# Softmax denominators moved from the probabilities to the outputs, by way of rows in memory, in a hybrid attention and state-space layer

## The chip, the cores and the metric

The kernel runs on one core of a Trainium2 chip. The metric is the device time of one execution in microseconds (us); lower is better.

## The reference, cut to what matters

One layer of a decoder works on 1024 prompt tokens and 8 x 4 sample tokens of width 1024. A normalised input goes through one projection, whose columns are the queries, keys and values of 16 attention heads of size 64, and the gate, the convolution input and the steps of a state-space mixer. Both mixers' outputs are joined, projected, and followed by a feed-forward part. The change touches only the prompt's attention. Its three dilated windows with merging weights amount to one softmax with a count of windows in the bias:

```python
m = jnp.max(logits, axis=-1, keepdims=True)
pr = jnp.exp(logits - m)
den = jnp.sum(pr, axis=-1)
o = jnp.einsum('gnhqk,gnkhd->gnqhd', pr, vb) / den    # per head, per query
```

The division can stand before the product with the values (on the probabilities) or behind it (on the output), since `den` belongs to a query and not to a key.

## The kernel before, in words

The program has four stages in one launch: `project` (queries, keys, values), `weave`, `mixers` (state-space scan and sample attention) and `outward` (output projection and feed-forward). The change lies in `weave`, in the ring of projection weights (`Ring`) that `weave` takes over from `project`, and in nothing else.

`weave` mixes two jobs by hand. Job one is the prompt's attention, head by head. Job two is the rest of the input projection: 20 feature tiles, 24 units of three matmuls each (`dense`, L973), the first 12 tiles followed by a four-tap convolution on VectorE (`convolve`, L1114 and L1118), all 20 by an activation (tanh on ScalarE, `gate` on VectorE, L1130). The order is written out in ticks, 12 for each head, from -9 to 193 and some more for the tail; every engine runs the same list of ticks in program order, so an instruction that waits holds up all behind it on its engine. With h the head and qt one of 8 tiles of 128 queries, a tick can hold:

- `scores(h, qt)` on TensorE (L991, L992), then `bias_min` on VectorE (L1078): adds the bias and takes each query's minimum into `att_min`; then, a tick later, `exponent` on ScalarE (L1172): the exponential with its sum into `att_den`.
- `invert` on VectorE (L1060), in the same tick as `exponent`: 96 instructions in all, each the inverse of one or two columns of `att_den`; then `normalise` on GpSimd (L920): multiplies the 128 x (128 to 1024) probabilities in place by a scalar of each query. GpSimd's queue also holds `split_part` (L233, L235), which cuts each raw weight tile into a high and a low part, two halves a tile, 3 and 5 ticks after the tile before it has begun on TensorE.
- `turn` on TensorE (L1002) transposes the probabilities; `keep_high` on ScalarE (L1180) and `keep_low` on VectorE (L1065) move them to memory in two parts; `values` on TensorE (L1017 to L1022) multiplies them with the values into one PSUM bank; `split_out` on ScalarE and `add_out` on VectorE (L1053) move the output of a half head into `att_oT`, 64 partitions a head; `store_out` on ScalarE's queue (L1203) writes a head's 64 x 1024 to memory.

Probabilities come out with queries on the partitions, so the inverse denominators are a column there. The outputs come out transposed, with queries along the free dimension, so there the same numbers must be a row, the same for all 64 partitions of a head.

SyncE's queue, also in ticks, loads keys, queries, bias, values and raw weights. Raw weights lie in a ring of two slots of 128 x 1024; tile n goes to slot n % 2 and its load waits until tile n - 2 has been split. Behind its last tick the same queue loads what `mixers` begins with (L1472, L1475, L1460 and on).

## Time and profile before

| | us |
|---|---|
| three runs | 1935.82, 1939.14 (median), 1946.28 |
| the profiled execution | 1942.02 |
| its span, first to last instruction | 1940.1 |
| stretch of `weave` in that span | about 330 to 830 |

The profile gives each engine's busy time and instructions by source line, what ended each idle time, and the chain of work that ended last. Engines: PE is TensorE's matmul, PEld its weight load, DVE VectorE, ACT ScalarE, POOL GpSimd, SP SyncE; a name with q behind it is that engine's own sequencer or queue. Granted clock is TensorE's, 1.00 being 2.4 GHz. Matmuls overlap, so their durations added up are more than the time that they take.

### The profile page before, as it was taken

How to read it: one execution, taken by the hardware profiler on the slowest of the kernel's cores; microseconds unless marked ns; L12 is line 12 of the kernel's file. 1: busy time of each engine (PE TensorE's matmuls, PEld its weight loads, DVE VectorE, ACT ScalarE, POOL GpSimd, SP SyncE). 2: the span in 40 equal slices, each digit the busy share in tenths (PEclk: the TensorE clock that was granted, in tenths of full speed). 3: DMA queues.
4: the chain of work that ended last, by engine and by line, in shares of the span. 5: the costliest groups of instructions: out<-in, count | busy, mean ns of one | idle time of the engine just before them, and what ended most of it. 6: DMA issues, size and time to landing. Idle time of an engine off the chain costs nothing.

```text
span 1940.1 us, 33409 instructions
## 1 busy us (share of the span) xinstructions
PE 1851.5 (95%) x12776; PEld 1700.9 (88%) x12776; DVE 1405.9 (72%) x1897; ACT 887.6 (46%) x1610; POOL 1099.8 (57%) x846
## 2 busy tenths in 40 slices
PE   8999999998888999989997999999999999999999
PEld 7999999887777888855556789989999999999999
DVE  5788830787677766569987655798767779877876
ACT  5433412576566777456663002343333344444442
POOL 4588740777676777424444223335555557777774
PEclk9999999999999999979998999999999999999999
DMA  4444433543443443389995535114343357444442
GB/s 172 148 169 179 172 136 94 126 130 95 109 110 95 134 125 111 113 287 327 328 319 177 185 145 189 73 61 183 123 162 144 137 212 285 149 152 156 143 134 92
DMA packets 139097, 309.31 MB, mean 159 GB/s; under 512 B 31659, under 2 KB 65323, under 8 KB 135228
## 3 DMA queue, kind: packets, MB, share of 16 engines
q1 hardware_dynamic: 114924, 270.60, 41.5%
q10 hardware_dynamic: 24016, 36.58, 5.5%
q8 instruction: 103, 1.69, 0.3%
q14 instruction: 54, 0.44, 0.1%
HBM read 222.42 MB, written 93.28 MB: 163 GB/s over the span
## 4 chain that ended last, share of the span: by engine, by line
PE 58%; DVE 11%; POOL 5%; issue 5%; ACT 3%; DMA 0%; ACTq 0%; DVEq 0%; POOLq 0%
PE ff_ps L2594 31%; PE dense_ps L973 7%; PE wo_psa L2429 5%; POOL att_p L920 3%; PE att_t_ps L1002 2%; PE wo_psb L2561 2%; PE wo_psa L2561 1%; PE att_s_ps L991 1%; PE att_s_ps L992 1%; DVE sa_vlo L1961 1%; POOL w_lo L235 1%; PE ssd_in L1638 1%; DVE silu_half L1118 1%; PE sa_s L1551 1%; DVE ssd_m L1879 1%
## 5 line engine op out<-in xcount | busy, mean ns | idle before, releaser
L2594 PE MATMUL ff_ps<-ff_set,ff_wring 128*128 128x264 f32 x5376 | 661.5, 286 | 8.4 <-DVE ff_set L3206 3.5
L2594 PEld LDWEIGHTS ff_ps<-ff_set,ff_wring 128*128 128x128 f32 x5376 | 658.9, 189 | 10.5 <-DVE ff_set L3206 3.9
L920 POOL TENSOR_SCALAR att_p<-att_p,att_rden 128x128 f32<-128x128 f32 (+7 forms) x128 | 242.3, 1901 | 118.2 <-DVE att_rden L1060 118.1
L2263 POOL TENSOR_TENSOR ff_wring<-const,ff_wring 128x256 fp32r<-128x256 f32 (+1 forms) x192 | 212.6, 1111 | 146.5 <-ACT ff_wring L2759 145.9
L2759 ACT ACTIVATE ff_wring<-const 128x256 fp32r<-128x256 f32 (+1 forms) x192 | 93.5, 489 | 222.0 <-PE ff_ps L2594 108.4
L3228 DVE TENSOR_TENSOR h<-h,ff_ps 128x528 f32<-128x528 f32 x192 | 133.2, 700 | 49.9 <-PE ff_ps L2594 47.1
L1180 ACT ACTIVATE att_pThi<-att_t_ps 128x512 fp32r<-128x512 f32 x192 | 93.5, 487 | 133.6 <-PE att_t_ps L1002 125.3
L1078 DVE CUSTOM_DVE_ANT_0 att_p<-att_s_ps,att_bias 128x128 f32<-128x128 f32 (+7 forms) x128 | 95.3, 754 | 57.8 <-PE att_s_ps L992 51.9
L1065 DVE TENSOR_TENSOR att_pTlo<-att_t_ps,att_pThi 128x512 fp32r<-128x512 f32 x192 | 104.5, 552 | 41.2 <-ACT att_pThi L1180 41.0
L973 PE MATMUL dense_ps<-u_hi,w_hi 128*128 128x352 f32 x480 | 115.0, 341 | 10.3 <-DVE conv_pre L1092 3.1
L2263 POOL TENSOR_TENSOR ff_wring<-wo_raw,ff_wring 128x256 fp32r<-128x256 f32 (+1 forms) x72 | 83.5, 1159 | 61.8 <-ACT ff_wring L2759 61.8
L680 DVE RECIPROCAL proj_rinv<-proj_rinv 128x1056 f32<-128x1056 f32 x16 | 108.1, 6753 | 9.8 <-ACT proj_rinv L570 9.8
L1002 PE MATMUL att_t_ps<-const,att_p 128*128 128x128 f32 x576 | 96.7, 277 | 13.3 <-POOL att_p L920 8.7
L973 PE MATMUL dense_ps<-u_hi,w_lo 128*128 128x352 f32 x480 | 108.8, 335 | 0.0
L973 PE MATMUL dense_ps<-u_lo,w_hi 128*128 128x352 f32 x480 | 107.7, 333 | 0.0
L1172 ACT ACTIVATE att_p<-att_p,att_min 128x128 f32<-128x128 f32 (+7 forms) x128 | 98.3, 769 | 12.9 <-DVE att_min L1078 12.5
L235 POOL TENSOR_TENSOR w_lo<-w_raw,w_hi 128x512 fp32r<-128x512 f32 (+1 forms) x52 | 100.2, 1928 | 5.4
L2253 POOL CAST wo_hi<-wo_raw 128x1024 fp32r<-128x1024 f32 x16 | 18.1, 1131 | 147.4 <-issue 83.4
L2263 POOL TENSOR_TENSOR ff_wring<-ff_raw,ff_wring 128x256 fp32r<-128x256 f32 (+1 forms) x72 | 78.0, 1083 | 40.0 <-ACT ff_wring L2759 40.0
L973 PEld LDWEIGHTS dense_ps<-u_hi,w_hi 128*128 128x128 f32 x480 | 81.2, 191 | 19.6 <-issue 11.3
L1002 PEld LDWEIGHTS att_t_ps<-const,att_p 128*128 128x128 f32 x576 | 70.4, 142 | 31.1 <-issue 20.4
L2429 PE MATMUL wo_psa<-mix_split,wo_hi 128*128 128x352 f32 x384 | 81.8, 341 | 7.3 <-DVE mix_split L2893 4.3
(366 smaller groups left out, 4316.2 us busy)
## 6 DMA issues: line engine op xcount, KB each, us to landing
tmp_r_sets<-h SPq DMA_DIRECT2D x16, 1848.0 KB, 5.9
ff_setraw<-tmp_r_sets SPq DMA_DIRECT2D x56, 528.0 KB, 5.5
sa_k<-in_cache_k SPq DMA_DIRECT2D x32, 640.0 KB, 8.9
sa_v<-in_cache_v SPq DMA_DIRECT2D x40, 512.0 KB, 4.7
w_raw<-in_w_feat SPq DMA_DIRECT2D x36, 512.0 KB, 6.4
out_qk<-proj_out SPq DMA_DIRECT2D x16, 528.0 KB, 8.0
tmp_bias_rows<-tmp_table ACTq DMA_DIRECT2D x8, 1024.0 KB
att_bias<-tmp_bias_rows SPq DMA_DIRECT2D x16, 512.0 KB, 3.4
```

The costliest lines, as they stand in the source:

```text
L235: pool.tensor_tensor(self.lo[:, j, ks, :], raw, self.hi[:, j, ks, :].bitcast(F32), ALU.subtract).then_inc(self.split, 2 // parts)
L680: dve.reciprocal(rinv[:], rinv[:]).then_inc(inverted, 1)
L920: pool.tensor_scalar(slot(h, qt), slot(h, qt), rden[:, qt, :], None, ALU.mult).then_inc(normed, 1)
L973: mm = pe.matmul(bank(acc, c, w), wt[:, j, k, :], xt[:, k, c:c + w], start=(k == 0 and p == 0), stop=(k == KD - 1 and p == 2))
L1002: mm = pe.transpose(t_ps[n % 2][:, c:c + P], slot(h, qt)[:, b * P:(b + 1) * P], kit.c(C_IDENT, P))
L1065: dve.tensor_tensor(p_lo[:, n % TURNED, off:512], t_ps[n % 2][:, off:512], p_hi[:, n % TURNED, off:512].bitcast(F32), ALU.subtract).then_i ...
L1078: dve.tensor_tensor_reduce(out=slot(h, qt), in0=s_ps[:, base:base + w], in1=bias[:, h % 2, SEQ - w:SEQ], scale=1.0, scalar=3e38, op0=ALU.a ...
L1172: act.activation(slot(h, qt), slot(h, qt), ACT.Exp, bias=low[:, qt, :], scale=-1.0, accum_out=den[:, qt, :]).then_inc(exped, 1)
L2263: pool.tensor_tensor(w_set(n)[:, 1], operand(q, m), w_set(n)[:, 0].bitcast(F32), ALU.subtract).then_inc(fw_split, 1)
L2429: mm = pe.matmul(bank(acc_a, c, w), wt[:, o % 2, k, :], xt[:, k, c:c + w], start=(k == 0 and wt is w_hi and xt is m_hi), stop=(k == KD - 1 ...
L2594: mm = pe.matmul(ff_ps[:, (b + g) * 512:(b + g) * 512 + HG], ws[:, wi, k, :], xs[:, xi, k, g * HG:(g + 1) * HG], start=(opens and k == 0 a ...
L3228: dve.tensor_tensor(two(block), two(block), out, ALU.add).then_inc(d_added, 1)
```

## The change

`normalise` goes: the probabilities stay unnormalised, and `turn` waits for the exponentials. `invert` becomes one VectorE instruction a head, at tick 12h + 2, for all eight columns. After each odd head the two heads' inverses go to memory as two rows of 1024 (`store_inverse`, on SyncE's queue), and four ticks later each row is loaded onto 64 partitions (`load_inverse`, two DMAs on the same queue). They land in slot 1 of the raw weight ring, which is given up after tile 17; tiles 18 to 35 share slot 0. When both heads of a pair are in `att_oT`, at tick 12h + 14 for the odd head h, one VectorE instruction multiplies its 128 x 1024 by those rows (`scale_out`), and the two stores of the pair follow a tick later.

```diff
+ONE_RAW = QK_TILES + 2
+    def place(self, n):
+        return n % 2 if n < ONE_RAW else 0
     def load(self, eng, dram, n):
         if n >= 2:
-            eng.wait_ge(self.split, max(2 * (n - 1), 3))
-        eng.dma_start(self.raw[:, n % 2, :], ...
+            eng.wait_ge(self.split, 2 * n if n > ONE_RAW else max(2 * (n - 1), 3))
+        eng.dma_start(self.raw[:, self.place(n), :], ...
...
+    pair_ends = {n: h // 2 for n, (h, g) in ends.items() if h % 2 and g}
+    inverts = {TICKS * h + 2: h for h in range(NH)}
-        busy[n] += 0.16 * (n - 1 in score) + 0.69 * (n in ends) + ...
+        busy[n] += 0.69 * (n in ends) + ... + 1.25 * (n in pair_ends)
...
+            def store_inverse(f):
+                sp.wait_ge(inverted, 2 * f + 2)
+                sp.dma_start(dram["rden"][2 * f:2 * f + 2, :].rearrange("h (t p) -> p h t", p=P), rden[:],
+                             allow_slow_non_contiguous=True).then_inc(rden_stored, 16)
+            def load_inverse(f):
+                sp.wait_ge(rden_stored, 16 * (f + 1))
+                if f >= 1:
+                    sp.wait_ge(o_scaled, f)
+                else:
+                    sp.wait_ge(ring.split, 2 * ONE_RAW)
+                for j in range(2):
+                    sp.dma_start(rows_inv[j * HD:(j + 1) * HD, :],
+                                 dram["rden"][2 * f + j].partition_broadcast(HD)).then_inc(rows_loaded, 16)
+                if n in inverts and inverts[n] % 2:
+                    store_inverse(inverts[n] // 2)
+                if n - 4 in inverts and inverts[n - 4] % 2:
+                    load_inverse(inverts[n - 4] // 2)
...
-            def normalise(h, qt):
-                pool.wait_ge(inverted, rank(h, qt) + 1)
-                pool.tensor_scalar(slot(h, qt), slot(h, qt), rden[:, qt, :], None, ALU.mult).then_inc(normed, 1)
...
             def turn(n, h, g, b):
-                pe.wait_ge(normed, NT * h + HALF * (g + 1))
+                pe.wait_ge(exped, NT * h + HALF * (g + 1))
...
-                if h >= 2 and g == 0:
-                    dve.wait_ge(mix_stored[h % 2], 16 * (h // 2))
+                if h >= 2 and h % 2 == 0 and g == 0:
+                    dve.wait_ge(mix_stored[0], 16 * (h // 2))
+                    dve.wait_ge(mix_stored[1], 16 * (h // 2))
...
+            def scale_out(f):
+                dve.wait_ge(rows_loaded, 32 * (f + 1))
+                dve.wait_ge(o_kept, 4 * f + 4)
+                dve.tensor_tensor(oT[:], oT[:], rows_inv, ALU.mult).then_inc(o_scaled, 1)
+            def invert(h):
+                dve.wait_ge(exped, NT * (h + 1))
+                if h >= 2 and h % 2 == 0:
+                    dve.wait_ge(rden_stored, 16 * (h // 2))
+                dve.reciprocal(rden[:, h % 2, :], den[:, :, 0]).then_inc(inverted, 1)
...
             def exponent(h, qt):
                 act.wait_ge(biased, rank(h, qt) + 1)
+                if h >= 1 and RANK[qt] == 0:
+                    act.wait_ge(inverted, h)
...
-            def store_out(h):
-                act.wait_ge(o_kept, 2 * h + 2)
+            def store_out(f):
+                act.wait_ge(o_scaled, f + 1)
+                for j in range(2):
...
```

## Rows read from the trace of the kernel before

**Rows 1.** The profile's first line.

```profile
span 1940.1 us, 33409 instructions
```

**Rows 2.** Busy time by stretch: PE, PEld, DVE, ACT, POOL, then granted clock, DMA share, GB/s.

```profile
330.00:380.00 50.00, 48.45 (x295) 46.19 (x294) 28.39 (x61) 26.91 (x49) 30.14 (x27) 0.97 0.68 158
380.00:520.00 140.00, 126.76 (x750) 111.82 (x749) 105.05 (x216) 92.29 (x177) 104.70 (x68) 0.97 0.44 112
520.00:660.00 140.00, 123.88 (x756) 109.81 (x757) 108.41 (x222) 89.90 (x179) 99.86 (x67) 0.99 0.43 106
660.00:830.00 170.00, 165.31 (x1028) 146.78 (x1027) 104.17 (x238) 111.31 (x216) 102.17 (x75) 1.00 0.41 123
```

**Rows 3.** TensorE's waits, 330 to 830: us in total, times, longest.

```profile
PE att_t_ps L1002 <- POOL att_p L920: 8.7, 6, 2.2
PE att_s_ps L991 <- DVE att_min L1078: 8.7, 7, 2.1
PE att_t_ps L1002 <- issue: 4.5, 8, 0.8
PE dense_ps L973 <- DVE conv_pre L1092: 3.1, 3, 1.8
PE dense_ps L973 <- DVE silu_half L1103: 3.0, 3, 1.5
PE att_pv_ps L1017 <- ACT att_oparts L1168: 3.0, 4, 1.0
PE att_s_ps L991 <- ACT att_qlo L1192: 2.6, 6, 0.9
PE dense_ps L973 <- POOL w_lo L235: 1.1, 1, 1.1
```

**Rows 4.** Other engines' waits, 330 to 830.

```profile
POOL att_p L920 <- DVE att_rden L1060: 118.1, 47, 8.3
...
DVE att_rden L1060 <- ACT att_p L1172: 16.6, 32, 0.9
```

**Rows 5.** Groups by line, GpSimd, 330 to 830.

```profile
L920 POOL TENSOR_SCALAR att_p<-att_p,att_rden 128x128 f32<-128x128 f32 (+7 forms) x128 | 242.3, 1901 | 118.2 <-DVE att_rden L1060 118.1
```

**Rows 6.** Groups by line, VectorE, 330 to 830.

```profile
L1118 DVE SCALAR_TENSOR_TENSOR silu_half<-conv_pre,conv_taps,silu_half 128x1080 f32<-128x1080 f32 x36 | 54.8, 1523 | 0.0
```

**Rows 7.** Line L1060: ns min/median/max, first and last start.

```profile
L1060 DVE RECIPROCAL att_rden<-att_den x96: 146/156/168, 348.7 to 798.2; 128x1 f32<-128x1 f32 x64, 128x2 f32<-128x2 f32 x32
```

**Rows 8.** Timeline, single lines: start, us, instruction, idle time before it.

```profile
469.56 1.33 DVE L1118 SCALAR_TENSOR_TENSOR silu_half<-conv_pre,conv_taps,silu_half 128x1080 f32<-128x1080 f32 x1
469.74 3.86 POOL L920 TENSOR_SCALAR att_p<-att_p,att_rden 128x1024 f32<-128x1024 f32 x1 [0.28 <-DVE att_rden L1060]
...
486.88 0.30 PE L1002 MATMUL att_t_ps<-const,att_p 128*128 128x128 f32 x1 [2.11 <-POOL att_p L920]
...
734.19 2.85 POOL L920 TENSOR_SCALAR att_p<-att_p,att_rden 128x1024 f32<-128x1024 f32 x1 [0.31 <-DVE att_rden L1060]
```

**Rows 9.** Line L1903, in the stage after.

```profile
L1903 DVE TENSOR_TENSOR h<-h,ssd_z x8: 1208/1209/1225, 876.3 to 1040.4; 128x1024 f32<-128x1024 f32 x8
```

**Rows 10.** Line L1226, DMAs of 1024 runs of 16 bytes.

```profile
L1226 ACTq DMA_DIRECT2D tmp_xbc<-silu_half x12: 452/456/1068, 360.4 to 654.5; - x12
...
DMA to landing us min/median/max: 5.5/7.1/9.6
```

**Rows 11.** Line L1203, DMAs of 64 rows of 4 KB.

```profile
DMA to landing us min/median/max: 2.8/3.4/7.7
```

**Rows 12.** SyncE's queue at the end of the stage, timeline.

```profile
805.10 0.38 SPq L1472 DMA_DIRECT2D sa_q<-out_qk  x1
...
807.69 2.42 SPq L1460 DMA_DIRECT2D sa_k<-in_cache_k  x4
```

**Rows 13.** TensorE at the end of the stage, timeline.

```profile
825.05 2.21 PE L1528 MATMUL sa_s<-sa_k,sa_qdiag 128*64 128x512 f32 x12
```

**Rows 14.** The profile's list of DMA issues: KB each, us to landing.

```profile
sa_k<-in_cache_k SPq DMA_DIRECT2D x32, 640.0 KB, 8.9
```

More of the change, by code:

```diff
@@ L216, in __init__ @@
         self.made = kit.sems("proj_made")
+    def place(self, n):
+        return n % 2 if n < ONE_RAW else 0
     def load(self, eng, dram, n):
         if n >= 2:
-            eng.wait_ge(self.split, max(2 * (n - 1), 3))
-        eng.dma_start(self.raw[:, n % 2, :], dram["w_feat"][n]).then_inc(self.loaded[n % 2], 16)
+            eng.wait_ge(self.split, 2 * n if n > ONE_RAW else max(2 * (n - 1), 3))
+        eng.dma_start(self.raw[:, self.place(n), :], dram["w_feat"][n]).then_inc(self.loaded[n % 2], 16)
     def split_part(self, kit, pool, n, half, parts):
         j, ks = n % 2, slice(half * KD // parts, (half + 1) * KD // parts)
-        raw = self.raw[:, j, :].rearrange("p (k m) -> p k m", k=KD)[:, ks, :]
+        raw = self.raw[:, self.place(n), :].rearrange("p (k m) -> p k m", k=KD)[:, ks, :]
         if half == 0:
@@ L798, in weave @@
         busy[n] += sum(0.18 + 0.134 * (qt + 1) for _, qt in score.get(n, ()))
-        busy[n] += 0.16 * (n - 1 in score) + 0.69 * (n in ends) + 0.7 * (n % TICKS == 9)
+        busy[n] += 0.69 * (n in ends) + 0.7 * (n % TICKS == 9) + 1.25 * (n in pair_ends)
     for d in range(ND):
@@ L830, in weave @@
         p_hi, p_lo = sb("att_pThi", [P, TURNED, 512], F32R), sb("att_pTlo", [P, TURNED, 512], F32R)
-        low, den, rden = sb("att_min", [P, NT, 1]), sb("att_den", [P, NT, 1]), sb("att_rden", [P, NT, 1])
+        low, den, rden = sb("att_min", [P, NT, 1]), sb("att_den", [P, NT, 1]), sb("att_rden", [P, 2, NT])
         o_parts, oT = sb("att_oparts", [HD, 2, 512]), sb("att_oT", [P, SEQ])
@@ L846, in weave @@
             "qkloaded", "vloaded", "qkcast", "vcast", "vsplit"))
-        (scored, biased, exped, inverted, normed, flipped, hi_kept, lo_kept, multiplied, o_split, o_kept) = (
-            kit.sems(f"att_{n}") for n in ("scored", "biased", "exped", "inverted", "normed", "flipped", "hi", "lo",
-                                           "multiplied", "osplit", "okept"))
+        (scored, biased, exped, inverted, flipped, hi_kept, lo_kept, multiplied, o_split, o_kept, o_scaled) = (
+            kit.sems(f"att_{n}") for n in ("scored", "biased", "exped", "inverted", "flipped", "hi", "lo",
+                                           "multiplied", "osplit", "okept", "oscaled"))
+        rden_stored, rows_loaded = kit.sems("att_rdenstored"), kit.sems("att_rows")
+        rows_inv = ring.raw[:, 1, :]
         mix_stored = kit.sems("mix_stored", 2)
@@ L944, in _ @@
             for n in range(FIRST - 1, END + 1):
-                for h, qt in score.get(n - 1, ()):
-                    normalise(h, qt)
                 for d in evict_at.get(n - 1, ()):
@@ L1054, in add_out @@
                                   o_parts[:, 1, :], ALU.add).then_inc(o_kept, 1)
-            def invert(tiles):
-                (h, first), n = tiles[0], len(tiles)
-                dve.wait_ge(exped, rank(h, first) + n)
-                dve.reciprocal(rden[:, first:first + n, 0], den[:, first:first + n, 0]).then_inc(inverted, n)
+            def scale_out(f):
[7 more added lines that the diff above has]
+                dve.reciprocal(rden[:, h % 2, :], den[:, :, 0]).then_inc(inverted, 1)
             def keep_low(n, h, g, b):
@@ L1153, in _ @@
                     split_v(h)
-                if n - 1 in score:
-                    invert(score[n - 1])
+                if n in pair_ends:
+                    scale_out(pair_ends[n])
+                if n in inverts:
+                    invert(inverts[n])
                 for d, t in tap_at.get(n, ()):
@@ L1199, in cast_v @@
                                ACT.Copy).then_inc(v_cast, 1)
-            def store_out(h):
-                act.wait_ge(o_kept, 2 * h + 2)
-                act.dma_start(dram["mix"][h * HD:(h + 1) * HD, :], oT[h % 2 * HD:(h % 2 + 1) * HD, :]
-                              ).then_inc(mix_stored[h % 2], 16)
+            def store_out(f):
+                act.wait_ge(o_scaled, f + 1)
+                for j in range(2):
+                    h = 2 * f + j
+                    act.dma_start(dram["mix"][h * HD:(h + 1) * HD, :], oT[j * HD:(j + 1) * HD, :]).then_inc(mix_stored[j], 16)
             def tanh(d):
@@ L1266, in _ @@
                     tanh(d)
-                if n - 1 in ends and ends[n - 1][1] == 1:
-                    store_out(ends[n - 1][0])
+                if n - 1 in pair_ends:
+                    store_out(pair_ends[n - 1])
                 for d in store_at.get(n, ()):
@@ L3462 @@
             "bias_sample": (NH * T_DEC, NKEY), "qk_low": (2 * D, SEQ), "cum_rows": (NT * NH, P), "part": (D, NTOK),
-            "hid": (D, NTOK), "r_sets": (UP_PAIRS * P, NP * HN)}
+            "rden": (NH, SEQ), "hid": (D, NTOK), "r_sets": (UP_PAIRS * P, NP * HN)}
 def kernel(**inputs):
```

## Prediction

> **What bounds the kernel now.** I read the profile from the outside in. The first line gives the span, 1940.1 us [rows 1]; the profiled execution took 1942.0 us, so 1.9 us lie around it, and it is 2.9 us above the median of the three runs, 1939.1. My sum is made against 1942.0 and moved down by 2.9 at the end. The change lies between 330 and 830 us, so I cut that stretch in four and looked at each engine's busy time [rows 2]. TensorE is the bound nearly everywhere: it is busy 464.4 of 500 us. VectorE has 346 us, GpSimd 337 us. So the stage cannot give back more than TensorE's idle time, about 35 us, and what a lower clock costs. The reader should see where the idle time lies: 13.2 us in 380 to 520, 16.1 us in 520 to 660, but 4.7 us in the last 170 us, although GpSimd is still 0.60 busy there (0.75 and 0.71 before). What ends between the third and the fourth stretch is the convolution on VectorE, whose share falls from 0.77 to 0.61. The stalls therefore come from VectorE and GpSimd together.
>
> Next, TensorE's own waits, which must be the same 35 us [rows 3]: they add up to 34.7. I sort them by who was late. GpSimd, normalising: 8.7. GpSimd, splitting weights: 1.1. VectorE: 8.7 + 3.1 + 3.0, and 4.5 more where nothing visible released a transpose that otherwise waits only for VectorE's keep_low, together 19.3. ScalarE: 3.0 + 2.6 = 5.6. This sorting is the main result: the largest item that is removed, 242.3 us of GpSimd work in 128 instructions [rows 5], is worth 8.7 us of TensorE's time directly, because GpSimd itself sat idle 118.1 us in front of it for want of inverses [rows 4]. A busy engine is not a late one.
>
> **Removed.** (1) 128 normalisations, 242.3 us [rows 5], all on GpSimd. The last line of defence is a transpose that waits for the last tile of a head; in one place it stood 2.11 us [rows 8]. In the changed kernel it waits for ScalarE's exponential, which is over before the inverse and the GpSimd pass even start, by the order of ticks three or more before TensorE needs it. I count all 8.7 us as gained. (2) 96 small inverses on VectorE, 96 x 0.156 = 15.0 us [rows 7], and VectorE's waits for ScalarE in front of them, 16.6 us [rows 4]; both hold up everything behind them in VectorE's queue.
>
> **Added on VectorE.** 16 inverses of eight columns. No such row exists; one and two columns cost nearly the same, 146 to 168 ns [rows 7], so I take 0.2 us, bounds 0.16 and 0.4: 3.2 us. Each waits for the last exponential of its head, but a tick later than before, so I take no wait for it. Eight products of 128 x 1024 from two memory operands; the same form takes 1.209 us in the next stage [rows 9]: 9.7 us. Semaphore turns in front of them, about 0.1 us each: 1 us. VectorE's queue thus loses 15.0 + 16.6 - 3.2 - 9.7 - 1 = 17.7 us of work and waiting over the stage.
>
> How much of the 19.3 us of VectorE's lateness goes with that? Bounds are nothing and all. Those waits are 21 single ones of at most 2.1 us [rows 3], so a queue that is 17.7 us lighter in 500 (about 1.1 us a head) touches many of them; but half of the relief is waiting for ScalarE, and an in-order engine often finds the next wait right behind the one that is gone. I take 45%, 8.5 us. Of ScalarE's 5.6 us I take 1 (bounds 0 and 5.6).
>
> Against this, where the GpSimd stall goes, TensorE reaches the next late partner earlier; that partner is VectorE. I take back 3 us (bounds 0 and 8.7).
>
> **The clock.** The granted clock was 0.97 in 380 to 520, which is 0.03 x 140 = 4.2 us of work at full rate [rows 2]; TensorE had its stalls there. With half of the stalls gone I count half, 2 us (bounds 0 and 4.2).
>
> **The round trip through memory.** SyncE stores 2 x 1024 inverses as 2048 separate elements of 4 bytes. The nearest row is a DMA of 1024 runs of 16 bytes: 5.5 to 9.6 us to landing, median 7.1 [rows 10]. Bounds: 7.1 if size decides, 19.2 (2 x 9.6) if the count does; I take the count at the median, 14.2 us. Then two loads of 64 rows of 4 KB, like the stores of the output: 3.4 us, at worst 7.7 [rows 11]. Together 17.6, at worst 27 us. What covers it: the inverse is made at tick 12h + 2, the product stands at tick 12h + 14, and a tick lasts 449.5 / 188 = 2.39 us (first inverse at tick -7, last at tick 181 [rows 7]), so 28.7 us. I cost the round trip at nothing, with 11 us of cover at my values and about 2 at the worst ones. The same cover holds for VectorE's inverse of the next even head, which waits for the store. The pair's two stores are issued at tick 12h + 15 and waited for at 12h + 18: 7.2 us of cover against 3.4 and one issue; only the slowest landing, 7.7, would show. Nothing.
>
> The Trainium skill (DMA: Bandwidth & Descriptors, section Rules for kernel authors) says that a pattern without a contiguous last dimension is lowered to one descriptor for each element. This is what my count of 2048 assumes; no row here shows 4-byte elements. By that rule the sum stays; it speaks for 14.2 rather than 7.1.
>
> **Queues that the steps pass.** SyncE is held from tick 12h + 6 until the store has landed, at most some ticks. Behind it stand raw weights, values and bias, all needed at least three ticks later: nothing. With one raw slot, a load waits until the tile before it is split, but TensorE cannot have begun that tile without the split, and it takes over 8 ticks over it: nothing.
>
> The exception is the end. The last inverse is made about tick 182, 2.4 us after the last one now at 798.2 [rows 7], so the last store lands at 800.6 + 0.5 + 14.2 = 815 (808 to 820). Only behind it can SyncE issue the sample queries and keys, now issued at 805.1 and 807.7 to 810.1 [rows 12]. With two more issues they go out some 11 us later, to about 821, and land 8.9 us later [rows 14], near 830, where TensorE wants them from 825.05 [rows 13]. They then also share the memory with the first loads of the next stage. TensorE has other waits there, so not all of it shows: I take 3 us lost (bounds 0 and 7). One more product and one more store issue in the tail: 0.5 us.
>
> **The sum.** 8.7 + 8.5 + 1 + 2 - 3 - 3 - 0.5 = 13.7 us gained. 1942.0 - 13.7 = 1928.3; less 2.9 this is 1925.4, so 1925 us.
>
> **Rivals.** First, VectorE is freed more than I think (time about 1911). GpSimd and VectorE hold each other up: a 1024-wide normalisation took 3.86 us when a two-operand product ran beside it and 2.85 us without one [rows 8], and the convolution's products average 1.523 us where an undisturbed one took 1.33 [rows 6, 8], 36 x 0.19 = 6.9 us lost on VectorE in the stretch where it is late. With 128 of GpSimd's passes gone, most of that returns. Then VectorE's 19.3 us and ScalarE's 5.6 nearly vanish: 8.7 + 19.3 + 5.6 + 2 - 7 (what remains) = 28.6, less 0.5 at the end: 28. Against it: the weight splits, which collide just as well, stay. The Trainium skill (SBUF — State Buffer, section Who interferes with whom) states this as a rule: a VectorE instruction with two operands in SBUF and a GpSimd instruction that reads SBUF exclude each other for a whole instruction. The 1.0 us difference above agrees with it.
>
> Second, VectorE takes over (about 1934). GpSimd's 8.7 us go but are waited for again on VectorE, which is 0.77 busy there: 8.7 - 4 + 4 - 3.5 = 5 us gained, within what can be told. For it: GpSimd was late only where VectorE had been. Against it: the queue does get 17.7 us lighter.
>
> Third, slower: the round trip. If 4-byte elements cost more than their count against 16-byte runs, the product waits in VectorE's queue with everything behind it. It decides when store and loads together pass 28.7 us, so a store of about 24 us. At 35 us each pair is late by some 11 us, of which TensorE can hide little: 8 x 9 = 72 us lost, near 1990; slower by 0.5% overall needs only 3 to 4 us a pair. Against it: twice the slowest 16-byte DMA is 19.2 us.
>
> Fourth, the change does not do what it says in time: the GpSimd pass was hidden altogether, and the end of the stage costs its full 7 us; no change, about 1939. The 2.11 us wait speaks against it.
>
> **Chances and range.** My forecast 0.50, with a range of its own of 1916 to 1932; more freed 0.16; VectorE takes over 0.15; no change 0.07; round trip or end slower 0.12. A measurement of this kernel tells about 0.5%, 9.7 us, from no change, so 1929.4 and 1948.8 are the limits. A part of the forecast's own range lies above the first. Faster 0.62, within 0.5% 0.25, slower 0.13. The range reaches from the case of more relief to just short of no change: 1908 to 1938.
>
> **What would show it.** In the profile after: no GpSimd line on the probabilities and none in TensorE's waits for its transposes; VectorE's waits for the inverse down from 16.6 us to a few; TensorE's waits for VectorE near 14 us; eight products near 1.2 us without a wait for a DMA in front; the store's landing between 7 and 19 us; sample keys issued after 810 with a wait on TensorE or VectorE just behind the stage. The prediction is wrong if VectorE waits for the rows, if the 19.3 us stay whole or vanish, or if the held keys cost more than 7 us.

## The result and the profile after

| | us |
|---|---|
| changed kernel, median of 8 runs | 1948.11 (1942.27 to 1950.27) |
| kernel before, median of 8 runs on the same chip | 1940.74 (1935.82 to 1946.28) |
| ratio, 95% interval | 1.003 (1.0016 to 1.0044) |
| profiled execution, its span | 1949.94, 1948.1 |

The changed kernel is not faster. By the ratio it is slower by 0.3%, about 6 us: less than the 0.5% that the prediction takes for what can be told, but outside the range of 1908 to 1938. The question is where the expected 14 us went, and 6 more.

Busy time by stretch, answering to [rows 2] (PE, PEld, DVE, ACT, POOL, then granted clock, DMA share, GB/s):

```profile
330.00:380.00 50.00, 48.17 (x292) 44.85 (x291) 29.03 (x57) 28.11 (x51) 9.61 (x14) 0.98 0.79 159
380.00:520.00 140.00, 126.38 (x729) 111.79 (x728) 101.85 (x189) 87.17 (x171) 29.62 (x30) 0.94 0.48 109
520.00:660.00 140.00, 130.16 (x788) 114.96 (x788) 108.59 (x207) 95.01 (x186) 25.21 (x30) 0.99 0.63 124
660.00:830.00 170.00, 163.47 (x991) 147.41 (x993) 101.93 (x209) 109.45 (x213) 23.29 (x27) 0.97 0.51 119
```

GpSimd's work on the probabilities is gone (its 337 us are now 88), and from 520 to 660 TensorE is busier by 6 us, as hoped. From 380 to 520 it is not, and its clock is lower, 0.94 against 0.97; so is that of the last stretch, 0.97 against 1.00. Call (1 - clock) x length the rate lost: 1.0 + 8.4 + 1.4 + 5.1 = 15.9 us, where before it was 1.5 + 4.2 + 1.4 + 0 = 7.1.

TensorE's waits from 330 to 830 (us in total, times, longest), answering to [rows 3]:

```profile
PE att_t_ps L1024 <- issue: 10.1, 7, 3.8
PE att_s_ps L1013 <- DVE att_min L1106: 5.1, 5, 1.9
PE att_s_ps L1013 <- ACT att_qlo L1224: 4.7, 10, 0.9
PE dense_ps L995 <- DVE conv_pre L1120: 3.6, 3, 1.8
PE dense_ps L995 <- POOL w_lo L240: 3.3, 1, 3.3
PE dense_ps L995 <- DVE silu_half L1131: 2.5, 2, 1.4
PE att_pv_ps L1039 <- ACT att_oparts L1198: 1.2, 1, 1.2
```

They sum to 30.5 us; before it was 34.7. The 8.7 us of waits for GpSimd's normalisation are gone. In their place the first row has grown from 4.5 to 10.1 us, and its longest from 0.8 to 3.8. It is the transpose, which can only be waiting for VectorE's `keep_low`. So I asked what VectorE waited for, from 330 to 830:

```profile
DVE silu_half L1142 <- DMA tmp_xbc<-silu_half: 15.7, 3, 6.4
...
DVE silu_half L1131 <- DMA tmp_xbc<-silu_half: 2.6, 1, 2.6
```

This is a wait that the change does not touch. L1142 is the first tap of the convolution; it writes into `silu_half` and must wait until ScalarE's queue has stored the features of the tile before from there. In the kernel before the same wait (L1114) took 1.9 us in all. And the stores themselves, L1258 (512 KB) and L1259 (1024 runs of 16 bytes), the latter answering to [rows 10]:

```profile
L1258 ACTq DMA_DIRECT2D tmp_xbc<-silu_half x12: 321/326/338, 357.4 to 651.3; - x12
...
DMA to landing us min/median/max: 2.8/6.0/13.7
...
L1259 ACTq DMA_DIRECT2D tmp_xbc<-silu_half x12: 448/464/1621, 357.8 to 651.6; - x12
...
DMA to landing us min/median/max: 5.7/8.4/17.8
```

The second took 9.6 us at most before. The worst case, in the timeline of the queues and then of VectorE and TensorE (start, us, instruction, idle time before it):

```profile
395.13 0.38 SPq L904 DMA_DIRECT2D tmp_rden<-att_rden  x1
400.31 0.33 ACTq L1258 DMA_DIRECT2D tmp_xbc<-silu_half  x1
400.67 0.79 ACTq L1259 DMA_DIRECT2D tmp_xbc<-silu_half  x1
407.12 1.16 SPq L914 DMA_DIRECT2D w_raw<-tmp_rden  x2
408.32 0.59 SPq L227 DMA_DIRECT2D w_raw<-in_w_feat  x1
...
418.57 0.88 DVE L1142 TENSOR_SCALAR silu_half<-conv_pre,conv_taps 128x1080 f32<-128x1080 f32 x1 [6.40 <-DMA tmp_xbc<-silu_half]
419.38 0.27 DVE L1093 TENSOR_TENSOR att_pTlo<-att_t_ps,att_pThi 128x128 fp32r<-128x128 f32 x1
...
419.75 0.52 PE L1024 MATMUL att_t_ps<-const,att_p 128*128 128x128 f32 x3 [3.78 <-issue]
```

Read it downwards. At 395.13 the store of 2048 single inverses is issued; SyncE, which waits for its landing, goes on at 407.12, 12.0 us later (the eight took 11 to 14 us, as estimated). At 400.67, in the middle of it, the feature store is issued on another queue. It lands at 418.5. VectorE stands 6.40 us, `keep_low` stands behind it in VectorE's queue, and TensorE stands 3.78 us behind that. The chain of work of this head says the same in one row:

```profile
400.67 17.78 DMA tmp_xbc<-silu_half
```

And the clock pays after the stall (stretches of 5 us, columns as above):

```profile
415.00:420.00 5.00, 1.22 (x10) 0.99 (x8) 1.43 (x3) 0.06 (x1) 1.65 (x2) 1.00 0.24 64
420.00:425.00 5.00, 4.36 (x20) 4.13 (x19) 5.00 (x6) 2.72 (x5) 3.47 (x3) 0.57 0.26 84
425.00:430.00 5.00, 5.00 (x26) 4.72 (x26) 4.06 (x8) 4.89 (x8) 0.21 (x1) 0.75 0.06 23
```

TensorE, nearly idle from 415 to 420, works again at a mean granted clock of 0.57 and then 0.75, that is for much of these 10 us at the lower of its two levels, 1.2 and not 2.4 GHz.

This is one wait of four. The others, with what TensorE did behind two of them:

```profile
366.97 0.84 DVE L1142 TENSOR_SCALAR silu_half<-conv_pre,conv_taps 128x1080 f32<-128x1080 f32 x1 [4.87 <-DMA tmp_xbc<-silu_half]
...
444.79 1.05 DVE L1142 TENSOR_SCALAR silu_half<-conv_pre,conv_taps 128x1080 f32<-128x1080 f32 x1 [4.41 <-DMA tmp_xbc<-silu_half]
446.54 0.41 PE L1024 MATMUL att_t_ps<-const,att_p 128*128 128x128 f32 x2 [3.39 <-issue]
...
648.54 1.08 SPq L914 DMA_DIRECT2D w_raw<-tmp_rden  x2
649.66 0.58 SPq L227 DMA_DIRECT2D w_raw<-in_w_feat  x1
651.65 0.45 ACTq L1259 DMA_DIRECT2D tmp_xbc<-silu_half  x1
662.90 1.39 DVE L1131 SCALAR_TENSOR_TENSOR silu_half<-dense_ps,x_rinv 128x352 f32<-128x352 f32 x3 [2.63 <-DMA tmp_xbc<-silu_half]
663.57 1.43 PE L995 MATMUL dense_ps<-u_hi,w_hi 128*128 128x352 f32 x3 [3.26 <-POOL w_lo L240]
```

They do not all have a 4-byte store beside them. The one at 367 comes before the first of these stores is issued. At 431.58, when the feature store is issued that ends the wait of 4.41 us, the first 4-byte store has landed (407.12) and the second is not yet issued (463.82); keys and queries are loaded beside it, from 430.78 on. At 651.65 the 4-byte store has just landed, and the rows and the raw weights that stood behind it in SyncE's queue are under way. TensorE's 3.26 us there are put down to GpSimd's split of the weights, but VectorE's late eviction (L1131) frees the PSUM bank at about the same moment; with longer runs in the store, the first experiment below, the same matmul waits 0.53 us, for L1131 alone, and does not wait for the split. So each of TensorE's three long stalls, 3.78, 3.39 and 3.26 us, stands behind a wait for a feature store, and the granted clock fell after each: to 0.80 and 0.52 in the stretches 445 to 450 and 450 to 455, and the same from 660 to 665 and 665 to 670.

### The profile page after: what moved, and what is told of

It is laid out like the page before. It is cut to its first block, busy times and chain, and to the rows that moved or that the text cites. A ratio compares the mean times of both kernels' runs of the same rounds, so it can differ in the third digit from the quotient of the medians.

```text
span 1948.1 us, 33232 instructions
## 1 busy us (share of the span) xinstructions
PE 1855.9 (95%) x12776; PEld 1703.9 (87%) x12776; DVE 1404.0 (72%) x1825; ACT 887.6 (46%) x1610; POOL 853.5 (44%) x718
## 4 chain that ended last, share of the span: by engine, by line
PE 60%; DVE 10%; issue 4%; ACT 4%; DMA 3%; POOL 1%; ACTq 0%; DVEq 0%; POOLq 0%
PE ff_ps L2627 31%; PE dense_ps L995 9%; PE wo_psa L2462 5%; PE att_t_ps L1024 2%; PE wo_psb L2594 2%; DMA tmp_xbc<-silu_half 2%; PE att_s_ps L1013 2%; PE att_s_ps L1014 1%; PE wo_psa L2594 1%; PE att_pv_ps L1041 1%; PE att_pv_ps L1039 1%; PE ssd_in L1671 1%; DVE sa_vlo L1994 1%; DVE ssd_m L1912 1%; PE sa_s L1584 1%
## 5 line engine op out<-in xcount | busy, mean ns | idle before, releaser
L238 POOL CAST w_hi<-w_raw 128x512 fp32r<-128x512 f32 (+1 forms) x52 | 45.8, 880 | 206.7 <-DMA w_raw<-in_w_feat 142.8
L1024 PE MATMUL att_t_ps<-const,att_p 128*128 128x128 f32 x576 | 96.5, 277 | 10.4 <-issue 10.1
L240 POOL TENSOR_TENSOR w_lo<-w_raw,w_hi 128x512 fp32r<-128x512 f32 (+1 forms) x52 | 90.1, 1733 | 5.2 <-POOL w_hi L238 0.2
L457 PE MATMUL proj_ps<-u_hi,w_hi 128*128 128x352 f32 x384 | 83.7, 326 | 4.0 <-POOL w_lo L253 4.0
```

Source lines behind the costliest of these rows:

```text
L1024: mm = pe.transpose(t_ps[n % 2][:, c:c + P], slot(h, qt)[:, b * P:(b + 1) * P], kit.c(C_IDENT, P))
```

## The experiments

Theory A: the store of 2048 elements of 4 bytes occupies the DMA engines, the convolution's feature stores land late because of it, and VectorE's first tap, which waits for them, stalls TensorE and costs clock. Rivals: the product or the wait for the rows costs VectorE more than it gives back; SyncE's queue, held until the store lands, brings other loads late; the one raw slot; the end of the stage. Every ratio is to the kernel before, timed on the same chip, with its 95% interval; one hundredth of a per cent is 0.19 us. The last column is read from the one profiled execution of each kernel.

| kernel | median us | ratio | VectorE's waits for feature stores, us |
|---|---|---|---|
| changed | 1948.11 | 1.003 (1.0016 to 1.0044) | 15.7 + 2.6 |
| longer runs in the store | 1926.62 | 0.9927 (0.9912 to 0.9942) | 4.3 |
| no round trip | 1925.2 | 0.9918 (0.9899 to 0.9937) | 6.6 |
| before + 8 stores | 1943.45 | 1.0012 (1.0 to 1.0024) | 6.4 |
| before, one raw slot | 1943.45 | 1.0014 (1.0001 to 1.0027) | 4.1 |
| rows loaded 3 ticks later | 1943.56 | 1.0009 (0.999 to 1.0029) | 12.5 + 2.4 |
| inverses turned on TensorE | 1934.48 | 0.9968 (0.9949 to 0.9987) | 11.0 |
| last rows behind sample loads | 1944.56 | 1.0014 (0.9996 to 1.0031) | 12.1 + 3.0 |
| before, no normalisation | 1935.22 | 0.9967 (0.9951 to 0.9983) | 4.3 |
| longer runs, strided product | 1933.14 | 0.996 (0.9947 to 0.9974) | 7.6 |
| gate in place | 1931.46 | 0.9943 (0.9927 to 0.9958) | 0 |
| before + 8 stores, later | 1958.78 | 1.0086 (1.0067 to 1.0105) | 9.2 |
| strided product, gate in place | 1924.35 | 0.9903 (0.9887 to 0.9918) | 0 |
| before, gate in place | 1940.0 | 0.9989 (0.9973 to 1.0004) | 0 |
| longer runs, gate in place | 1920.89 | 0.9896 (0.9877 to 0.9915) | 0 |
| before + later stores, gate in place | 1948.76 | 1.003 (1.0015 to 1.0045) | 0 |

### Longer runs in the store

```diff
-                sp.dma_start(dram["rden"]....rearrange("h (t p) -> p h t", p=P), rden[:], ...
+                sp.dma_start(dram["rden"]....rearrange("h (p t) -> p h t", p=P), rden[:]
```

> The changed kernel, but the inverses are stored in 128 runs of 64 bytes instead of 2048 single elements; the rows then hold the inverses in another order, so the outputs of the attention are scaled wrongly, at the same cost. Theory A (the 4-byte stores hold the DMA engines for 11 to 14 us, the convolution's stores land late behind them, VectorE waits for these, TensorE stalls and its clock falls): VectorE's waits for the store of its feature rows fall from 18.3 us to about 2, the stage 330 to 830 shortens by 12 to 16 us against the changed kernel, total 1926 to 1934. Theory B (one raw weight slot and GpSimd waiting for raw weights are the cost): unchanged within 3 us, about 1947. Theory C (VectorE is the bound and takes over what GpSimd gave back): at most 5 us better than the changed kernel, about 1943.

The runs are 256 of 32 bytes, not 128 of 64 as this text says. Measured 1926.62 us: 20 us quicker than the changed kernel by the two ratios, with the same instructions on every engine. The rows hold the inverses in another order, so the outputs are scaled wrongly. In its timeline SyncE goes on 4.4 us after the store is issued (12.0 in the changed kernel):

```profile
397.08 0.38 SPq L904 DMA_DIRECT2D tmp_rden<-att_rden  x1
401.50 1.18 SPq L914 DMA_DIRECT2D w_raw<-tmp_rden  x2
```

The feature stores (L1259) land in time again:

```profile
DMA to landing us min/median/max: 5.4/6.9/9.6
```

And the stretch that was bad (columns as above):

```profile
380.00:520.00 140.00, 132.92 (x812) 117.24 (x812) 114.69 (x214) 97.88 (x191) 31.58 (x33) 1.00 0.50 129
```

TensorE is 132.9 us busy in place of 126.4, and its clock is back at 1.00. The form of this one DMA is the cause; the products, the raw slot and the order at the end of the stage are all still there. What this run does not tell apart is what the form does: it loads the DMA engines, and it holds SyncE's queue. Of the waits for feature stores 3.72 us are left at 369, again ahead of the first store of inverses.

### No round trip at all

Store, loads and product taken out; `o_scaled` is raised by VectorE without them.

> The changed kernel without the store of the inverses, without the loads of the rows and without the eight products: the attention's output is left undivided. The single raw slot stays. This is the whole of what moving the division can give back. Theory A: 1919 to 1927, that is the 13 to 20 us that I had forecast for the removed work plus 4 us for the end of the stage. Theory B: stays near 1943, since the slot is still single. Theory C: 1935 or above.

1925.2 us: the same as with the longer runs. So the eight products on VectorE, the row loads and the wait for them cost nothing that these runs can tell. VectorE waits 3.99 and 2.65 us for feature stores here, though no inverse is stored at all.

### The stores alone, on the kernel before

```diff
+                if n >= TICKS + 2 and (n - TICKS - 2) % (2 * TICKS) == 0:
...
+                    sp.dma_start(dram["rden"]....rearrange("h (t p) -> p h t", p=P), extra[:], ...
```

> The kernel before, all its work kept, with eight added stores of 2048 single elements of 4 bytes from a constant tile, on SyncE's queue at the tick where the changed kernel has them; the last one is waited for before the sample loads, as there. Theory A: 8 to 18 us slower than before (1949 to 1959), with VectorE's wait for the feature stores up from 1.9 us to over 8 and sample keys 10 us late. Theory B and theory C: within 3 us of before (1938 to 1944), except for up to 4 us at the end of the stage.

0.1%, 2 us: far too little for theory A as it stood. The trace shows why it may be: the first of the stores is issued at 393.08 and the feature store at 402.35, 9.3 us apart instead of 5.2, so that little was left to collide with. A later experiment moves the stores. But nearness is not the whole of it: the second and the third of these stores go out at 453.65 and 514.60, 1.4 and 0.5 us ahead of a feature store, and VectorE waits 2.3 us and nothing. What counts too is how soon VectorE wants the buffer.

### One raw slot alone, on the kernel before

`place` and the longer wait of `load`, nothing else.

> The kernel before with one raw weight slot for tiles 18 to 35, nothing else. Theory A, and my argument in the prediction (TensorE cannot begin a tile before it is split, so the load's new wait costs nothing): within 2 us of before. Theory B: 6 us slower or more, with waits of TensorE for w_lo above the 1.1 us of before.

0.14%, 2 to 3 us, with the lower bound of the interval next to nothing. TensorE's wait for a split is 1.1 us, as before.

### The rows loaded three ticks later

```diff
-                if n - 4 in inverts and inverts[n - 4] % 2:
-                    load_inverse(inverts[n - 4] // 2)
+                if n - 7 in inverts and inverts[n - 7] % 2:
+                    load_inverse(inverts[n - 7] // 2)
```

> The changed kernel, but SyncE issues the loads of the rows seven ticks after the store instead of four, when the store has long landed: the 4-byte stores still hold the DMA engines, but SyncE's queue is held less. If the harm is in the DMA engines (theory A): within 3 us of the changed kernel, 1944 to 1950, VectorE still waits 15 us or more for feature stores. If the harm is in SyncE's held queue (raw weights issued late, TensorE's 3.3 us for w_lo, then a clock drop): 5 us or more faster, 1943 or below.

The edit does not do what the expectation says of it. SyncE comes to the loads later in its list but not in time, and stands there until the store has landed:

```profile
397.15 0.38 SPq L904 DMA_DIRECT2D tmp_rden<-att_rden  x1
403.42 0.76 SPq L227 DMA_DIRECT2D w_raw<-in_w_feat  x1
408.93 1.23 SPq L914 DMA_DIRECT2D w_raw<-tmp_rden  x2
```

That is 11.8 us, where the changed kernel had 12.0. What moved is one load of raw weights, which no longer stands behind the hold. The ratio falls by 0.2%, within the intervals, and VectorE's waits for the feature stores are nearly all still there (12.5 + 2.4). So this run says little on the held queue; the kernel before with later stores (below) says more.

### The inverses turned on TensorE

TensorE transposes the 128 x 16 inverses, VectorE copies them out, and the store has 16 runs of 512 bytes, for seven of the eight pairs; the last pair keeps the old store.

> A version meant to beat both: the inverses of a pair (128 x 16) are transposed by TensorE in a free part of the score bank, copied by VectorE (16 x 128) and stored in 16 runs of 512 bytes, for seven of the eight pairs; the last pair keeps its 4-byte store, but its rows are loaded behind the sample loads. Theory A: no wait of VectorE for feature stores above 2 us, 1922 to 1932, faster than before by 0.4 to 0.9%. If VectorE is the bound: its eight copies of about 0.25 us and the waits around them leave it at 1938 or above.

0.9968. Better than the changed kernel by 0.6%, but not by the full 1.0%: VectorE gets 4.2 + 2.3 us of waits for the transposes, and its waits for feature stores, 11.0 us, did not fall as they should. Two of them, 5.8 us at 367 and 5.1 at 440, stand far ahead of the only 4-byte store, that of the last pair. This is a miss of theory A. The changed kernel has the same two waits, 4.87 at 367 and 4.41 at 445, and there too no 4-byte store is under way. The first is in every version of the changed kernel whose first tap can wait for feature stores (3.7 to 5.8 us). The second varies, from none in the run above and 0.59 us with longer runs to 5.1 here, with keys and queries loaded beside the feature store each time; what makes it long is not shown.

### The end of the stage

The last pair's rows are loaded behind the sample queries, keys and bias.

> The changed kernel, but the rows of the last pair are loaded behind the sample's queries, keys and bias instead of in front of them. If the held sample loads cost what I took from the traces (sample queries issued at 816.7 instead of 805.1, about 4 us behind the stage): 3 to 5 us faster than the changed kernel, 1943 to 1945. If the end costs nothing: unchanged, 1948.

The sample queries went out at 798.2 instead of 816.65, and it gave 0.16%, 3 us, with overlapping intervals: the size that the prediction had put on the end, and no more than a hint.

### The kernel before without the normalisation

```diff
-                for h, qt in score.get(n - 1, ()):
-                    normalise(h, qt)
...
-                pe.wait_ge(normed, NT * h + HALF * (g + 1))
+                pe.wait_ge(inverted, NT * h + HALF * (g + 1))
```

> The kernel before with only GpSimd's normalising pass taken out: transposes wait for the inverses, which VectorE still makes 96 times; the output is left undivided. It prices the GpSimd pass alone. My prediction's terms (8.7 us of direct waits and 2 of clock, less 3) give 1932; if the port that GpSimd shares with VectorE matters as well, 1925; if the pass was hidden, 1939.

0.33%, 6.4 us. The convolution's products fell from a mean of 1523 ns [rows 6] to 1365 with GpSimd's passes gone, 5.7 us less VectorE work. The rest of what the change could give, 0.49% up to the run with no round trip, lies in what else those two kernels differ in, mainly VectorE's 96 small inverses, the waits in front of them, and the transposes that wait for them. No run takes these apart.

### The whole computation with longer runs

```diff
+                by_tile = oT[:].rearrange("q (t p) -> q t p", t=NT)
+                dve.tensor_tensor(by_tile, by_tile, rows_inv.rearrange("q (p t) -> q t p", t=NT),
+                                  ALU.mult).then_inc(o_scaled, 1)
```

> The changed kernel with the inverses stored in 256 runs of 32 bytes, as in the run with longer runs, but the whole computation of the reference: the product reads the rows of inverses with a stride of 8 elements, so that each output column meets its own inverse. The theory of the 4-byte stores says that the gain of the run with longer runs stays whole, if the product's strided read costs no more than its plain one (1.22 us in the changed kernel): 1926 us, ratio to before 0.993, feature-store waits of VectorE under 5 us. If the strided read costs double (eight products of 2.4 us), VectorE is 9.6 us longer busy over the stage, of which by the prediction's 45% up to 4 us reach the end: 1930 us. The rival, that the run with longer runs was quick for another reason than its DMA pattern, such as the moved tick or chance placement, has no reason to give this kernel another time than it gave that one, but would show no relation to the feature-store waits.

```profile
L1083 DVE TENSOR_TENSOR att_oT<-att_oT,w_raw x8: 2023/2135/2289, 423.6 to 816.5; 128x1024 f32<-128x1024 f32 x8
```

Reading one operand with a stride of 32 bytes makes the product 2135 ns instead of 1225: 7.3 us of VectorE for the eight. It cost 0.33%, 6.4 us, more than the 4 us expected.

### Gate in place

```diff
-                    dve.scalar_tensor_tensor(out=half[:, 0:w], in0=th[:, 0:w], scalar=1.0, in1=half[:, 0:w],
+                    dve.scalar_tensor_tensor(out=th[:, 0:w], in0=th[:, 0:w], scalar=1.0, in1=half[:, 0:w],
...
-                        dve.wait_ge(feat_stored, stores(d))
+                        dve.wait_ge(activated, d)
...
-                    act.wait_ge(activated, d)
+                    act.wait_ge(feat_stored, stores(d))
...
-                    act.dma_start(rows[:, 0:SEQ], half[:, 0:SEQ]).then_inc(feat_stored, 16)
+                    act.dma_start(rows[:, 0:SEQ], th[:, 0:SEQ]).then_inc(feat_stored, 16)
```

> The changed kernel, its 4-byte stores as they are, with one step of the convolution moved: the gate writes its product over the tanh buffer and the features are stored from there, so VectorE's first tap of the next tile needs only the gate before it and no longer the landing of the stores; ScalarE's tanh of the next tile waits for that landing in its place, four taps (about 6 us of work and several ticks) later. Theory A, that the 4-byte stores delay the feature stores and the first tap's wait for them is what stalls the stage: the waits of VectorE at the first tap for the feature stores (15.7 + 2.6 us) go, the long waits of TensorE at the turns around 419 and 447 us go too, and the time falls most of the way to the run without the round trip: 1926 to 1934 us, ratio 0.993 to 0.997. The rival, that the same DMA load reaches the time by another way (the loads of weights, q, k or bias landing late, or the SP queue held): the first tap's waits go but the time stays at 1942 to 1948 us, ratio 1.001 to 1.004. If the waits return at the tanh, ScalarE shows waits for the feature stores, and the time lies between.

The same 4-byte stores, and 0.87% quicker than the changed kernel. The feature stores (L1259) are as late as ever, and nobody waits for them:

```profile
DMA to landing us min/median/max: 6.4/8.3/19.1
```

In VectorE's timeline a first tap follows its `keep_low` at once:

```profile
409.77 0.42 DVE L1093 TENSOR_TENSOR att_pTlo<-att_t_ps,att_pThi 128x256 fp32r<-128x256 f32 x1
410.10 0.83 DVE L1142 TENSOR_SCALAR silu_half<-conv_pre,conv_taps 128x1080 f32<-128x1080 f32 x1
```

And TensorE's waits for `keep_low`, 330 to 840 us:

```profile
PE att_t_ps L1024 <- issue: 1.7, 5, 0.9
```

1.7 us in place of 10.1, none over 0.9. So the waits at the first tap are worth 0.87%, 17 us, in the changed kernel. Not all of that is the 4-byte stores' doing, as the controls below show.

### The stores on the kernel before, at the changed kernel's moment

```diff
+                    sp.wait_ge(lo_kept, TICKS * (2 * f + 1) + 4)
```

> The kernel before with the eight stores of 2048 elements of 4 bytes again, as in the run that added them, but each issued two ticks later, where the changed kernel issues its own, some 5 us and not 9 us ahead of the feature stores. Theory A with the timing refinement (the cost hangs on how closely the 4-byte store and the feature store meet): the feature-store waits of VectorE rise from 6.4 us in the run with earlier stores to 10 to 18 us, and the time rises by 4 to 10 us over the kernel before: ratio 1.002 to 1.005. The rival, that stores alone are harmless to the kernel before and what matters is an interplay with the changed order of VectorE and GpSimd: ratio 0.999 to 1.0015, though the waits rise.

16.7 us lost, where the same stores two ticks earlier cost 2: more than any theory said. The first store now goes out at 399.28 (393.08 there) and the feature store at 402.91, 3.6 us apart, which is nearer still than the changed kernel's 5.2. SyncE waits for none of these stores but the last before it goes on, so a held queue is not needed for the harm. VectorE and TensorE in the timeline:

```profile
422.41 0.84 DVE L1128 TENSOR_SCALAR silu_half<-conv_pre,conv_taps 128x1080 f32<-128x1080 f32 x1 [7.55 <-DMA tmp_xbc<-silu_half]
...
423.55 0.87 PE L1016 MATMUL att_t_ps<-const,att_p 128*128 128x128 f32 x3 [4.96 <-issue]
```

And from the list of DMA issues, 330 to 840 us, with the median landing at the end:

```profile
w_raw<-in_w_feat SPq DMA_DIRECT2D x18, 512.0 KB, 10.4
```

Two things are late: the feature store, and the raw weights (10.4 us to landing, 6.3 in the kernel before). GpSimd waits 5.8 us for the weights, and in this kernel the normalisations stand behind its splits; TensorE's waits for them rise from 8.7 to 11.3 us.

### Both edits, and their controls

The strided product and the gate in place together:

> Both edits together on the changed kernel: stores of the inverses in runs of 32 bytes with the strided product, and the gate in place with the features stored from the tanh buffer. With the short stores gone only about 4 us of feature-store waits are left to take away, so the theory of the 4-byte stores says that the second edit adds little: 1922 to 1926 us, ratio 0.991 to 0.993, within 2 us of the kernel with the longer runs alone. The rival, that the gate in place is worth much by itself whatever the stores do (because VectorE waits at the first tap for other reasons also in the kernel before), says 1915 to 1920 us, ratio 0.987 to 0.989.

1924.35 us, ratio 0.9903: the best kernel that computes the whole reference, better than both. But it is 0.57%, 11 us, under the strided product alone, where 7.6 us of first-tap waits were taken away. Three controls for this:

> The kernel before with the gate in place alone: features stored from the tanh buffer, VectorE's first tap free of the feature stores. In that kernel VectorE waited 1.9 us for them. Theory A says that the edit is worth what such waits cost and nothing else: 1936 to 1943 us, ratio 0.998 to 1.001. The rival, raised by the kernel with both edits being 8.8 us quicker than the one with the strided product alone where at most 7.6 us of first-tap waits were to be had, says that the edit has a value of its own: 1930 to 1935 us, ratio 0.994 to 0.997.

> The changed kernel with the inverses stored in 256 runs of 32 bytes and read in memory order, so that the product costs 1.22 us again but the order of the inverses is not the reference's, and the gate in place. Left out is only that order. If the strided product's extra 0.9 us, eight times, is still felt once the first-tap waits are gone, this is 2 to 6 us quicker than the kernel with both edits and the stride: 1918 to 1922 us, ratio 0.988 to 0.990. If it is hidden (VectorE no longer late): 1923 to 1925 us, ratio 0.990 to 0.991.

> The kernel before with the eight 4-byte stores at the changed kernel's moment, which cost 16.7 us, and the gate in place. Theory A in its narrow form, that all of the cost runs through the first tap's wait for the feature stores: 1940 to 1946 us, ratio 0.999 to 1.002. In a wider form, that the 4-byte stores also hold the loads of raw weights (GpSimd waited 5.8 us for them in the stage, and the normalisations stand behind its splits in that kernel's queue): the cost falls only by the part of the first tap, 1947 to 1954 us, ratio 1.003 to 1.006. If the gate in place changes nothing here, 1955 us or more, the first tap is not the way.

The gate in place is worth 0.11% (the interval holds no change) on the kernel before, and 0.31% with the longer runs, where 4.3 us of waits went. So it has next to no value of its own, and the gain follows the waits: 2, 6, 11 and 17 us where 1.9, 4.3, 7.6 and 18.3 us of waits went. A wait of VectorE there costs about its own length, at times more. The strided product costs 0.07% with the gate in place by the ratios (3.5 us between the medians, taken on two chips), less than the 0.33% without it; the intervals leave open whether it is felt at all.

These runs also price the 4-byte stores a second time. With the gate in place, when nobody waits at the first tap, the form of the store still makes a difference: 0.9943 with single elements, 0.9896 with longer runs, so 0.47% or 9 us, give or take some 5 by the two intervals. Of the 20 us about 11 therefore go through the first tap and about 9 by other ways. The two profiled executions show where: from the first transpose to the last one 446.7 and 437.1 us, with TensorE's waits in that stretch at 22.5 and 17.0 us and its clock at 0.99 and 1.00; from there to the last product of the state-space stage 227.4 and 223.3 us. The second part goes with the end of the stage: the last store of inverses holds SyncE for 12.0 us in the one and 1.6 us in the other, and the first sample keys from the cache go out at 803.1 and 785.2.

On the kernel before with the later stores the edit gives back 0.56%, 10.9 of 16.7 us. What is left, 5.8 us, is there with no wait of VectorE for features at all; GpSimd's waits for raw weights (7.1 us) and TensorE's for GpSimd (12.4 us) are still there, so the wider form of the theory holds here.

## Why the prediction was wrong

**The failed step** is in the part on the round trip and the one on the queues. I costed the store by its own landing (14.2 us against a cover of 28.7) and by who waits for it, and wrote "Nothing". Its own landing was right: 11 to 14 us, and VectorE never waited for the rows. What I left out is what 2048 elements do to everyone else's transfers while they are under way, and to what stands behind them in SyncE's queue. The feature store, 7.1 us in [rows 10], took up to 17.8; the raw weights' landing rose from 6.3 to 8.3 (medians). I used [rows 10] as a price for the new store and did not ask who was waiting for that row. Cost: 1.03% between the changed kernel and the one with longer runs, 20 us. Of these about 11 run through the first tap: the gate in place gives 17 us in the changed kernel, but 6 of them also with the longer runs. The other 9 are there with nobody waiting at the first tap, some 4 of them behind the last transpose by the profiled executions.

**The third rival** named the round trip as the danger, with the wrong mechanism and point: it was to decide when store and loads together passed 28.7 us. The store cost 20 us with the rows well inside their cover.

**The sum without that step was right in total, in part by luck.** 13.7 us forecast; with longer runs the ratio gives 0.73%, 14.2 us, and without a round trip 15.9. The terms missed in both directions:

- GpSimd's waits, 8.7 us: gone, as counted. Taking out the pass alone gives the kernel before 6.4 us.
- VectorE's lateness, 8.5 of 19.3 us (45% would be 8.7), less the 3 us taken back, so 5.5. In the kernel with longer runs TensorE's waits for VectorE in the stage are 4.2 + 3.1 + 3.0 + 1.6 = 11.9 us, so 7.4 went. The inverses of eight columns took 0.192 us (0.2 estimated), the products 1.225 (1.209).
- ScalarE, 1 of 5.6: none. The waits are 4.7 + 1.2 = 5.9 us in the changed kernel and 5.8 + 1.7 = 7.5 with longer runs.
- Clock, 2 us gained: in the changed kernel the sign was wrong. The rate lost rose from 7.1 to 15.9 us, some 10 of them right behind the three long stalls. With longer runs the term is right, and more: the rate lost is 1.5 + 0 + 1.4 in the first three stretches and nothing from 660 to 810, so 2.9 in place of 7.1. The 0.96 that the stretch from 660 to 830 shows there comes from 810 on (0.80, then 0.52), when the next stage has begun.
- The end, 3 us lost: the last store landed at 815.5 (815 forecast) and the keys went out at 820.6 (821). Moving them gave 3 us, too small for its interval. With longer runs they went out at 790.6, 10 us ahead of the last transpose (800.9), so there the term is not in the 14.2.
- One raw slot, nothing: 0.14% alone on the kernel before, an interval that nearly reaches no change. A small miss at most.

**First rival and the rule.** The Trainium skill (SBUF — State Buffer, section Who interferes with whom) says that a VectorE instruction with two inputs in SBUF and a GpSimd instruction that reads SBUF keep each other out. The trace agrees: 1523 ns a convolution product before, 1412 in the changed kernel, 1365 in the kernel before without the pass. But the rival wanted nearly all of VectorE's and ScalarE's lateness gone, and with longer runs 11.9 and 7.5 us of it are there.

**Still open:** what makes the feature stores of 357 and of some 425 to 431 land late enough to be waited for, with no 4-byte store near, in the changed kernel and in the one with transposed inverses; and how the 9 us that do not go through the first tap split between raw weights, keys, queries and bias and the held queue.

## What to carry to other kernels

A DMA of many tiny elements is to be priced twice: by its own landing, and by what the transfers of all other queues lose meanwhile; list the transfers in flight beside it and ask which engine waits for each, and in which buffer. A wait that costs 2 us today because a transfer takes 7 is the first to grow. Where a buffer is rewritten right after it is stored, let the store read another buffer that is needed later: here that took another output operand, a slightly wider tanh buffer and three moved waits. And before a wait is put down to a suspect, look whether it is there already when the suspect is not.

## What was not expected of the hardware

- 2048 elements of 4 bytes took 11 to 14 us from issue until SyncE went on behind them, 256 runs of 32 bytes 1.6 to 5.2 us to landing (median 2.9), for the same 8 KB.
- A store of 512 KB and one of 1024 runs of 16 bytes, issued 5 us behind it on another queue, landed after up to 13.7 and 17.8 us; in the kernel before the medians were 3.4 and 7.1. A landing of 13.1 us came with no 4-byte store near (issued at 431.58).
- The same eight stores on the kernel before cost 2 us or 16.7, by a shift of two ticks, 6 us at the first of them.
- A two-operand VectorE product of 128 x 1024 with one operand at a stride of 8 elements took 2135 ns, plain 1225.
- After a TensorE stall of 3.78 us the granted clock was 0.57, then 0.75, in the next two stretches of 5 us; after one of 3.26 us it was 0.52 from 665 to 670.
